# Interleaving the loads, transposes and splits of the input's quarters with the low-rank group's units at the head of a two-layer trunk

## What is computed

```
h = x                                             # (256, 2048)
y = x * rsqrt(mean(x*x) + 1e-6) * ev_norm         # RMS norm
z = y @ ev_w_in                                   # (2048, 7456)
z_ret, z_rw = z[:, :4096], z[:, 4096:]            # retention; RWKV: r, k, v and the low-rank inputs
r, k, v, wl, al, gl = split(z_rw, [1024]*3 + [64, 64, 160])
```

## Time and profile before

| | |
|---|---|
| median of three runs | 2407.71 us |
| the profiled execution | 2406.72 us, span 2405.0 us |
| granted clock of PE, mean | 0.996 |
| PE busy | 2352.6 us, 98% of the span |
| DVE, ACT, POOL busy | 1468.4, 1099.2, 235.2 us |
| bytes moved | 411.64 MB, mean 171 GB/s |

### The profile page before, as it was taken

How to read it: one execution, slowest core, us unless ns; L and a number is a source line. 1 busy time by engine, 2 the same in 40 slices (tenths; PEclk the granted TensorE clock), 3 DMA queues, 4 the chain that set the end, 5 groups by cost and what they waited for, 6 DMA issues and landing times.

```text
span 2405.0 us, 36954 instructions
## 1 busy us (share of the span) xinstructions
PE 2352.6 (98%) x14242; PEld 1965.9 (82%) x14242; DVE 1468.4 (61%) x1645; ACT 1099.2 (46%) x1405; POOL 235.2 (10%) x184
## 2 busy tenths in 40 slices
PE   7999999999999999999999999989999999999997
PEld 7877777777888888888888888878888888888886
DVE  5456666755566566566566566775665665665664
ACT  5444444434444344344344445754543443443443
POOL 0002114421000000000000001220000000000001
PEclk9999999999999999999999999999999999999999
DMA  7653332333566666665665665555666666666654
GB/s 222 187 155 102 91 96 85 102 96 125 184 183 192 193 184 191 194 185 191 193 191 186 191 202 167 159 172 186 183 192 194 185 190 195 185 191 193 187 191 157
DMA packets 215462, 411.64 MB, mean 171 GB/s; under 512 B 13264, under 2 KB 19792, under 8 KB 215184
## 3 DMA queue, kind: packets, MB, share of 16 engines
q1 hardware_dynamic: 213888, 406.94, 55.1%
q0 software_dynamic: 1424, 2.49, 0.3%
HBM read 407.28 MB, written 2.10 MB: 170 GB/s over the span
## 4 chain that ended last, share of the span: by engine, by line
PE 93%; DVE 3%; ACT 2%; issue 1%; POOL 0%; DMA 0%; SPq 0%; DVEq 0%; ACTq 0%
PE acc_pair L226 19%; PE acc_pair L227 18%; PE acc_pair L228 18%; PE acc_pair L242 10%; PE tp_pair L242 10%; PE tp_pair L244 5%; PE acc_pair L244 5%; PE tp_pair L773 5%; PE acc_pair L773 1%; PE tp_pair L367 1%; DVE stg L724 1%; PE acc_pair L1578 1%; PE tp_pair L1578 1%; ACT L766 0%; DVE w_lo L215 0%
## 5 line engine op out<-in xcount | busy, mean ns | idle before, releaser
L215 DVE TENSOR_TENSOR w_lo<-raw,w_hi 128x1024 fp32r<-128x1024 f32 (+1 forms) x760 | 1015.3, 1340 | 733.1 <-ACT w_hi L210 726.5
L210 ACT ACTIVATE w_hi<-raw 128x1024 fp32r<-128x1024 f32 (+1 forms) x760 | 800.9, 1055 | 905.8 <-PE acc_pair L228 578.8
L242 PE MATMUL acc_pair<-xT_both,w_hi 128*128 128x512 f32 x1024 | 320.7, 394 | 4.3 <-issue 2.9
L242 PE MATMUL tp_pair<-xT_both,w_hi 128*128 128x512 f32 x1024 | 317.2, 391 | 0.0
L226 PE MATMUL acc_pair<-w_hi,xT_both 128*128 128x512 f32 (+1 forms) x736 | 299.7, 407 | 4.3 <-DVE w_lo L215 4.3
L227 PE MATMUL acc_pair<-w_lo,xT_both 128*128 128x512 f32 (+1 forms) x736 | 285.1, 387 | 0.0
L228 PE MATMUL acc_pair<-w_hi,xT_both 128*128 128x512 f32 (+1 forms) x736 | 284.9, 387 | 0.0
L226 PE MATMUL acc_pair<-w_hi,hidA_hi 128*128 128x512 f32 x640 | 251.4, 393 | 6.3 <-DVE hidA_lo L1612 6.3
L226 PE MATMUL acc_pair<-w_hi,hidB_hi 128*128 128x512 f32 x640 | 250.6, 392 | 0.0
L227 PE MATMUL acc_pair<-w_lo,hidA_hi 128*128 128x512 f32 x640 | 250.4, 391 | 0.0
L228 PE MATMUL acc_pair<-w_hi,hidA_lo 128*128 128x512 f32 x640 | 250.1, 391 | 0.0
(11 more groups left out here) (240 smaller groups left out, 2386.8 us busy)
## 6 DMA issues: line engine op xcount, KB each, us to landing
raw<-in_ff_w SPq DMA_DIRECT2D x512, 512.0 KB, 4.4
raw<-in_ev_w_in SPq DMA_DIRECT2D x112, 512.0 KB, 3.7
raw<-in_od_w_in SPq DMA_DIRECT2D x64, 512.0 KB, 4.0
raw<-in_ev_w_out SPq DMA_DIRECT2D x32, 512.0 KB, 3.6
raw<-in_od_w_out SPq DMA_DIRECT2D x32, 512.0 KB, 4.5
raw<-in_ev_w_in SPq DMA_DIRECT2D x8, 288.0 KB, 5.6
x<-in_x_in SPq DMA_DIRECT2D x4, 512.0 KB, 7.1
gate_w<-in_gx_w SPq DMA_DIRECT2D x8, 256.0 KB, 2.8
```

Source lines behind the costliest of these rows:

```text
L210: act.activation(w_hi[:, j % RING, :, 0:wide], raw[:, j % RING, :, 0:wide], ACT.Copy).then_inc(hi_ready, 1)
L215: dve.tensor_tensor(w_lo[:, j % RING, :, 0:wide], raw[:, j % RING, :, 0:wide], w_hi[:, j % RING, :, 0:wide], ALU.subtract).then_inc(lo_rea ...
L242: nc.tensor.matmul(o[:, :], w_hi[:, j % RING, kt % KU, c * P:(c + 1) * P], both, start=(kt == 0), stop=False)
```

## The change

Only the head changes. Quarters 2 and 3 are no longer loaded and turned ahead of the low-rank group. SP loads quarter 2 after unit 1 and quarter 3 after unit 3. PE, ACT and DVE run the whole posts of quarters 0 and 1 first, then units 0 and 1, the post of quarter 2, units 2 and 3, the post of quarter 3, and units 4 to 7. PE's waits become four: before units 0, 2, 4 and 6 for `lhs_ready` 4, 8, 12 and 16. The squares keep their places, but after units 1 and 3 they stand behind the post. The number of instructions and of bytes is the same.

```diff
--- before.py
+++ after.py
@@ -571,7 +571,12 @@
                 return dve.tensor_copy(z_lora[:, 0:2, :], bank[:, :].rearrange("p (c t) -> p c t", c=2))
             return dve.tensor_copy(z_lora[0:32, 2, :], bank[0:32, 0:T])
 
-        LORA = dict(n=0, bank=0, post="z", wide=LORA_W, free=None, need=(12, 16), tused=2, stg=0, norm=1,
+        def lora_need(pe, j):
+
+            if j % 2 == 0:
+                pe.wait_ge(lhs_ready, 2 * j + 4)
+
+        LORA = dict(n=0, bank=0, post="z", wide=LORA_W, free=None, need=lora_need, tused=2, stg=0, norm=1,
                     tp=(lhs_ready, 16), move=lora_move)
 
         def rkv(i, odd):
@@ -1153,10 +1158,21 @@
                     pe_front_sum(eng, 0, acc[2])
                     pe_front_lora(eng, 0, acc[3])
 
-        def even_in(role, eng, prev, parts):
+        def load_x(sp, k):
+
+            sp.dma_start(x[:, :, k * WIDE:(k + 1) * WIDE],
+                         x_in[:, k * WIDE:(k + 1) * WIDE].rearrange("(h p) n -> p h n", p=P)).then_inc(x_landed[k], 16)
+
+        def even_in(role, eng, posts, parts):
+
+            prev = posts[-1]
 
             def first_norm(role, eng, j):
 
+                if role == "sp" and j in (1, 3):
+                    load_x(eng, 2 + j // 3)
+                elif role in ("pe", "act", "dve") and j in (1, 3):
+                    finish(role, eng, posts[2 + j // 3])
                 if role == "act":
                     if j in (1, 2, 3, 6):
                         k = min(j - 1, 3)
@@ -1167,7 +1183,7 @@
                     dve_variance_of_x(eng, prev)
                     dve_finish_norm(eng, prev, late=True)
 
-            step(role, eng, LORA, ev_w_in, 0, RET_IN + 3 * RET_W, xT, prev, first_norm)
+            step(role, eng, LORA, ev_w_in, 0, RET_IN + 3 * RET_W, xT, None, first_norm)
             if role == "sp":
                 eng.dma_start(con[:, P:], consts[:, P:]).then_inc(sem("masks_landed"), 16)
             step(role, eng, rkv(0, 0), ev_w_in, 0, RET_IN, xT, LORA)
@@ -1724,10 +1740,10 @@
 
         def program(role, eng):
             posts = load_posts("ev_norm")
-            for p in posts[:-1]:
+            for p in posts[:2]:
                 finish(role, eng, p)
             parts = [0, 0]
-            even_in(role, eng, posts[-1], parts)
+            even_in(role, eng, posts, parts)
             rwkv(role, eng, parts)
             prev = even_projection(role, eng)
             prev = mlp(role, eng, 0, C_MLP0, prev, "od_norm")
@@ -1741,11 +1757,9 @@
         def _(sp):
 
             sp.dma_start(ident, consts[:, CIDENT:CIDENT + P]).then_inc(tables_landed, 16)
-            for k in range(4):
-                sp.dma_start(x[:, :, k * WIDE:(k + 1) * WIDE],
-                             x_in[:, k * WIDE:(k + 1) * WIDE].rearrange("(h p) n -> p h n", p=P)).then_inc(x_landed[k], 16)
-                if k == 0:
-                    sp.dma_start(par[:, :], params).then_inc(tables_landed, 16)
+            load_x(sp, 0)
+            sp.dma_start(par[:, :], params).then_inc(tables_landed, 16)
+            load_x(sp, 1)
             program("sp", sp)
             sp.wait_ge(hid_ready, C_END["hid"])
             sp.wait_ge(t_done[0], C_END["tused"][0])

```

## The result

The changed kernel takes 2418.88 us (median of five runs, 2417.36 to 2420.35), against 2407.76 us before (2407.53 to 2409.07). The ratio is 1.0045, with a 95% interval of 1.0034 to 1.0056: 11 us slower. The profiled execution has a span of 2415.7 us against 2405.0, that is 10.7 more.

A forecast was written before the change was run, and what follows sets the result against it. The prediction took PE's chain, 93% of the span, to bound the kernel. Its terms, -3.0 + 0.8 + 9.5 + 2.6 = +9.9 us, gave a forecast median of 2417.6 us, range 2414.3 to 2420.4.

The forecast's parts named there:

- The start, -3.0: Head, unit 0: DVE begins `w_lo` at 14.22 instead of 17.23, so PE starts at about 15.1; -3.0 us.
- The waits, +9.5: Ahead of units 2 and 4: PE stands 4.77 us each while ACT does `xT_hi`, squares and split; +9.5 us.
- one more set of transposes, +0.8: Low-rank group on PE: two sets of eight transposes inside the stretch where one stood before; +0.8 us.
- my lower bound: Waits ahead of units 2 and 4 if the squares could be left out of ACT's row: 2 x 3.31 = 6.6 us.
- The clock, +2.6: Units 2 and 4 on PE: 24 matmuls run at the slow pace after the waits; +2.6 us, bounds nothing to +4.9.
- my rival with the longer slow stretches: PE's slow stretches in the head last as long as at 1590: +12.2 us, 2419.9; chance 0.15.
- my main band: Whole kernel: the forecast band of 2416.3 to 2418.8 us, given a chance of 0.60.
- The rival that the clock stays up: PE's clock does not fall in the waits ahead of units 2 and 4: +7.7 us, 2415.4; chance 0.16.
- Nothing for units 3, 5, 6, 7: Low-rank group: these units' splits cost PE nothing; unit 3 makes PE wait 0.4 us only if unit 2 is not slow.
- nothing for the loads: SP's queue: same DMAs, quarters 2 and 3 land long before they are needed; no cost.
- The rival on the other side: PE's waits ahead of units 2 and 4 are filled: +3.4 us, or -2.2 without waits; 0.09, including later work absorbing the shift.
- ACT's idle time: On ACT ahead of `xT_hi` of quarter 2: an idle stretch of about 6.9 us expected in the profile.

## Why the prediction was right

**The start, -3.0.** It measured -2.8 (15.29 for 18.12). DVE was free at the same point of its order; the 0.2 us are a later landing of the table `par` (PE starts at 6.30 and not 6.05).

**The waits, +9.5 and one more set of transposes, +0.8.** I put 5.57 us from PE's transposes to its next matmul, added up from five rows of before; it measured 5.57 both times, and again in the second profile. The profile counts 4.54 us of that as idle and I had 4.77, because it gives the transposes 1.03 us and I took the 0.80 us from the first of them to the next matmul. Together the two terms measured +10.3, as forecast. That ACT's row decides it, and DVE's is next at about 4.5, is shown by moving the squares: 4.42 and 4.41. So my lower bound, 2 x 3.31 us without the squares, was too low: it left out that DVE's row takes over, which makes it 2 x 3.6. (ACT also had six splits and not five ahead of the one exchange of the kernel before; nothing hangs on that.)

**The clock, +2.6.** I had every burst behind a wait start at half the clock. All four waits of 4.54 us, in two profiles, had 13 or more slow matmuls behind them, but only three of the four bursts started slow; the fourth began with three matmuls at the full pace. Filling the waits gave 2.65 us back. The size is not a fixed one: 40 slow matmuls in one profile of the changed kernel and 54 in the other, against the 36 that I put (12 in each of three stretches). The difference to the 12 of before is worth 3.1 or 4.6 us at 0.109 us each, and all 96 matmuls of the low-rank group took 3.3 or 4.8 us more than before (17.47 and 18.95 us for 14.16). This term is the one that was too small, and with it the sum: 9.9 forecast, 10.8 measured at the head in the first profile and 12.4 in the second. The first is near my sum, the second is my rival with the longer slow stretches (12.2). Both happen in the same kernel, so the choice between them was not one that the kernel decides, and that the first profile came so near to 9.9 is partly luck. The median, 2418.88, lies between the two forecasts (2417.6 and 2419.9), just above the upper edge of my main band, 2418.8. The rival that the clock stays up is out for waits of 4.54 us, though it did happen once behind one of 3.38.

**Nothing for units 3, 5, 6, 7, and nothing for the loads.** No wait is in the profile inside a pair, and the run with only the loads changed is that of before. With the waits filled and the pace full, unit 3 was late by some 0.25 us (0.4 forecast), and unit 5 not at all.

**The rival on the other side** (the exchanges are covered) is not what the changed kernel does, but it is what the transposes ahead of unit 0 make of it: no wait inside the group, and 2.0 us less than before at the next one. I had put the covered case at no better than -2.2.

**ACT's idle time** I put at 6.9 us and it was 8.48: ACT was done with the splits at 12.7 and not 13.9, since quarter 1 was turned right behind quarter 0 (one stretch of 16 transposes from 6.30, without the 0.99 us that PE had waited for x before), and PE's transposes of quarter 2 came 0.5 later. It changes nothing, since it was PE's turn.

## What to carry to other kernels

When two engines exchange work in a fixed order, look at what stands between the producer's instruction and the consumer's next one on the same engine: the engine that hands work out needs enough independent work behind it to last through the other engines' whole rows, here 5.6 us of them for 0.8 us of transposes. Here starting earlier, by splitting a preparation into pieces, paid only when each piece was handed out ahead of the work that covers it: 11 us were lost with it behind, and up to 2 us gained with it ahead. And whatever else stands in the row of the engine that returns the result, as the squares here, is part of the wait.

## What the runs showed of the hardware

A wait of PE cost more than its length here. Behind 4.54 us of idle time 13 to 18 matmuls of 288 columns ran 0.24 us apart in place of 0.13, in all four cases (granted clock 0.66 over each window of 5 us that holds them in the first profile, which mixes the levels of 1.2 and 2.4 GHz). Behind 3.38 us of idle time inside the group it was so in three of four cases (23, 23 and 14 matmuls), and once not at all.

The fall need not come during the wait. In two of these seven cases PE was already at work again, at the full pace, when it slowed: after three matmuls (0.47 us) behind a wait of 4.54 us, and after six (0.89 us) behind one of 3.38.

The same kernel had 40 slow matmuls in one execution and 54 in another. Dummy transposes in the wait kept the full pace (3.60 us for a pair of units against 4.76), in four of four waits.

The record of the granted clock is not to be trusted at the start. Over the first slow stretch (15 to 20 us) it reads 1.00 in the first profile of the changed kernel and 0.50 in the second, while the matmuls' pace shows the lower level in both.
